# A chain of two transformer blocks on one core: halved first loads and identity products in the opening, another way of normalizing at the end

## The chip, the core and the metric

One core of one Trainium2 chip. The metric is the device time of one execution in microseconds (us). The kernel before takes 1332.92 us, the median of three runs from 1332.46 to 1334.28.

## The reference, cut to what matters

The input x is 256 rows (tokens) of 1024 float32 values. Two blocks follow each other; all matrices are float32 and each is used once:

```python
x = first_block(x, ...)      # z = rms_norm(x, norm_g) @ w_in, retention, differential attention, w_out
h = x                        # second block, two layers
for layer in range(2):
    h = h + 0.5 * swiglu_ffn(rms_norm_2(h, ffn1_norm[layer]), ...)
    h = h + (conformer_conv(...) if layer < 1 else stick_breaking_attention(...) @ attn_w_o)
    h = h + 0.5 * swiglu_ffn(rms_norm_2(h, ffn2_norm[layer]), gate, up, down)
return rms_norm_2(h, final_norm)   # h * rsqrt(mean(h * h) + 1e-6) * g
```

The change touches the two ends: the road from x to the first products with w_in, and the road from the last products (the down matrix of the last ffn) through the last residual and the last rms norm to the output.

## The kernel before, in words

Products are made from pairs of float32r parts: a value is split into a rounded part (hi) and the remainder (lo), and three products hi·hi, lo·hi, hi·lo are summed in PSUM. The weights come as a stream of 208 slabs, each four 128-row tiles of 512 columns (1 MB, two DMAs of 512 KB on SP's queue, `load`), in a ring of four slots (`raw`, `whi`, `wlo`). For every slab ACT makes the rounded part (`cast`, line 1092, signal `hi_ready`), DVE the remainder (`low`, line 1384, signal `lo_ready`), each two slabs ahead of TensorE, and TensorE runs 24 products of 512 columns: four tiles, two token tiles t of 128, three parts (`slab`, `part`, lines 595 to 597). A slot is loaded again when its remainder is made and rounded again when TensorE has used it (`half_done`).

Opening. SP loads x in two DMAs of 512 KB (one for each token tile), then the slabs. ACT loads the gain of the first norm, TensorE transposes it (line 736). TensorE then waits for x and transposes it in four fills (`fill`, line 673), each four 128x128 transposes into one of the two banks `tp`; a fill gives two of the eight k tiles. ACT scales each by the gain and rounds it (`fill_hi`, line 1105), DVE makes the remainder (`fill_lo`, line 1399). A third fill needs the first one's remainder. Both engines do two fills, then slab 0, then two fills, then slab 1. The norm's root factor is applied to results later: DVE collects statistics of x after slab 1 (`stats_half`, `stats_close`) and POOL makes the root (`residual_rs`), after which POOL issues its small loads. The order of the first slabs is (chunk 0, lower k), (chunk 1, lower k), (chunk 0, upper k), (chunk 1, upper k), so slabs 0 and 1 need k tiles 0 to 3 alone, which are the left half of x. `GAIN_STEP`, `LAM_STEP` say at which slab the other gains and small vectors are used.

End. The last ffn (`ffn2b`) has 11 down slabs. The left 512 output columns are complete in the middle of slab 5; DVE adds them to h (`residual`, line 1433) and takes their statistics. The last slab holds four k tiles for the right 512 columns: 12 products for t = 0, then 12 for t = 1. For each t DVE adds the right half to h (line 1962), takes statistics of it and joins them (lines 1415 to 1971), POOL makes the root in two steps (lines 429 and 433), DVE multiplies both halves by root and gain (line 1978), and SP stores each half of a tile, four stores of 256 KB (line 404). SP ends when all have landed.

`KEEP_WARM` (line 955, in the middle of the kernel) is a block of 22 products of 128x128 float32 whose results nobody reads. At line 1281 ACT loads the table set of the square root, and lines 1292 and 1301 use Square and Sqrt.

## Time and profile before

| | us |
|---|---|
| median of three timed runs | 1332.92 |
| span of the profiled execution | 1330.2 |
| TensorE busy in it | 1306.7 (98%) |
| DVE busy | 873.8 (66%) |
| ACT busy | 625.0 (47%) |
| POOL busy | 100.3 (8%) |

The profiled execution's own time runs from its first to its last instruction, 1330.2 us, and is 2.7 us under the median of the timed runs; the rest lies around the span. A busy time adds up the instructions of an engine; TensorE's are pipelined, so their starts lie nearer together than they are long, and the distance of starts is what a product costs in a stream. The timeline gives start, duration, engine, line and operands, and in brackets how long the engine had been idle and what released it. The chain of waits goes back from the last instruction, each piece to what released it.

### The profile page before, as it was taken

What the parts mean: (1) busy time and instruction counts of PE and PEld (TensorE: products, weight loads), DVE (VectorE), ACT (ScalarE), POOL (GpSimd) and SP (SyncE); (2) the same over time, 40 slices, a digit from 0 to 9 for tenths busy, and PEclk for the clock granted to TensorE, in tenths of its full rate; (3) what the DMA queues carried; (4) which work ended last, traced back from release to release, by engine and by line L of the source; (5) the groups of instructions that cost most, each with busy time, mean ns of one, the idle gap of its engine ahead of it and who ended that gap; (6) DMA issues with size and microseconds to landing.
All of it is one profiled execution on the core that took longest, in us unless ns stands there. A gap on an engine that the chain in (4) does not pass through costs nothing.

```text
span 1330.2 us, 17856 instructions
## 1 busy us (share of the span) xinstructions
PE 1306.7 (98%) x7374; PEld 1130.3 (85%) x7374; DVE 873.8 (66%) x988; ACT 625.0 (47%) x760; POOL 100.3 (8%) x141
## 2 busy tenths in 40 slices
PE   7999999999999999999999999999999999999997
PEld 5888877888888888899888888998888887988886
DVE  5565676767677655886777755557775566777753
ACT  5255576524455533325455543345554355455540
POOL 4123011001000002110000000000000010100000
PEclk9999999999999999999999999999999999999999
DMA  9544535456656655310455574545556422565540
GB/s 317 164 165 162 178 127 154 163 191 198 211 181 194 209 192 195 127 64 1 159 172 190 188 235 165 190 159 186 190 188 228 159 96 83 186 218 190 186 166 32
DMA packets 164911, 224.82 MB, mean 169 GB/s; under 512 B 7473, under 2 KB 105857, under 8 KB 164832
## 3 DMA queue, kind: packets, MB, share of 16 engines
q1 hardware_dynamic: 163168, 220.23, 50.3%
q0 software_dynamic: 1648, 3.47, 1.0%
q8 instruction: 58, 0.95, 0.3%
q14 instruction: 21, 0.17, 0.0%
q10 hardware_dynamic: 16, 0.00, 0.0%
HBM read 222.62 MB, written 1.05 MB: 168 GB/s over the span
## 4 chain that ended last, share of the span: by engine, by line
PE 94%; DVE 3%; ACT 2%; DMA 0%; issue 0%; POOLq 0%; DVEq 0%; POOL 0%; SPq 0%; ACTq 0%
PE acc L652 14%; PE acc L595 14%; PE acc L597 14%; PE acc L596 14%; PE att L652 8%; PE acc L650 7%; PE att L650 4%; PE att L891 4%; PE acc L626 2%; PE acc L630 2%; PE acc L628 2%; PE tp L673 1%; ACT pre L1310 1%; DVE wlo L1384 1%; ACT whi L1092 0%; DVE wexp L1938 0%
## 5 line engine op out<-in xcount | busy, mean ns | idle before, releaser
L1384 DVE TENSOR_TENSOR wlo<-raw,whi 128x2048 fp32r<-128x2048 f32 x208 | 474.6, 2290 | 167.9 <-ACT whi L1092 167.8
L1092 ACT ACTIVATE whi<-raw 128x2048 fp32r<-128x2048 f32 x208 | 395.0, 1913 | 102.4 <-PE acc L597 92.2
L652 PE MATMUL acc<-aT,whi 128*128 128x512 f32 x832 | 290.9, 391 | 0.0
L650 PE MATMUL acc<-aT,wlo 128*128 128x256 f32 x832 | 233.6, 281 | 0.0
L652 PEld LDWEIGHTS acc<-aT,whi 128*128 128x128 f32 x832 | 155.6, 187 | 33.8
L595 PE MATMUL acc<-whi,aT 128*128 128x512 f32 x448 | 179.6, 401 | 3.7 <-DVE wlo L1384 2.0
L597 PE MATMUL acc<-wlo,aT 128*128 128x512 f32 x448 | 175.8, 392 | 0.0
L596 PE MATMUL acc<-whi,aT 128*128 128x512 f32 x448 | 175.7, 392 | 0.0
L652 PE MATMUL att<-aT,whi 128*128 128x512 f32 x448 | 157.8, 391 | 0.0
L650 PEld LDWEIGHTS acc<-aT,wlo 128*128 128x128 f32 x832 | 157.3, 189 | 0.0
L595 PE MATMUL acc<-whi,hT_hi 128*128 128x512 f32 x352 | 137.3, 390 | 0.0
L596 PE MATMUL acc<-whi,hT_lo 128*128 128x512 f32 x352 | 137.0, 389 | 0.0
L597 PE MATMUL acc<-wlo,hT_hi 128*128 128x512 f32 x352 | 136.9, 389 | 0.0
L650 PE MATMUL att<-aT,wlo 128*128 128x256 f32 x448 | 125.4, 280 | 0.0
L595 PEld LDWEIGHTS acc<-whi,aT 128*128 128x128 f32 x448 | 85.1, 190 | 22.2 <-issue 3.5
L597 PEld LDWEIGHTS acc<-wlo,aT 128*128 128x128 f32 x448 | 85.1, 190 | 18.1
L652 PEld LDWEIGHTS att<-aT,whi 128*128 128x128 f32 x448 | 83.8, 187 | 18.4
L596 PEld LDWEIGHTS acc<-whi,aT 128*128 128x128 f32 x448 | 85.2, 190 | 16.5
L1227 ACT ACTIVATE low_part<-acc 128x512 f32<-128x512 f32 x52 | 31.0, 596 | 124.4 <-PE acc L652 124.4
L1105 ACT ACTIVATE aT<-tp,gain 128x256 fp32r<-128x256 f32 x72 | 28.3, 475 | 123.4 <-PE tp L673 123.4
L650 PEld LDWEIGHTS att<-aT,wlo 128*128 128x128 f32 x448 | 84.7, 189 | 0.0
L597 PEld LDWEIGHTS acc<-wlo,hT_hi 128*128 128x128 f32 x352 | 66.1, 188 | 13.8
(306 smaller groups left out, 1737.7 us busy)
## 6 DMA issues: line engine op xcount, KB each, us to landing
raw<-in_ffn_w_gate_dram SPq DMA_DIRECT2D x88, 512.0 KB, 3.8
raw<-in_ffn_w_up_dram SPq DMA_DIRECT2D x88, 512.0 KB, 4.9
raw<-in_ffn_w_down_dram SPq DMA_DIRECT2D x88, 512.0 KB, 4.7
raw<-in_w_in_dram SPq DMA_DIRECT2D x72, 512.0 KB, 4.6
raw<-in_conv_w_pw_dram SPq DMA_DIRECT2D x24, 512.0 KB, 4.7
raw<-in_w_kv_dram SPq DMA_DIRECT2D x16, 512.0 KB, 5.0
raw<-in_ret_w_o_dram SPq DMA_DIRECT2D x8, 512.0 KB, 4.8
raw<-in_diff_w_o_dram SPq DMA_DIRECT2D x8, 512.0 KB, 4.4
```

What stands on the lines that cost most here:

```text
L595: mm_(banks[t][:, :], tokens(Th, kt, t), hi_, start=first_ and j == 0, stop=False)
L596: mm_(banks[t][:, :], tokens(Tl, kt, t), hi_, start=False, stop=False)
L597: last = mm_(banks[t][:, :], tokens(Th, kt, t), lo_, start=False, stop=last_ and j == len(kts) - 1)
L626: mm_(dst, whi[:, slot, cols], aT_hi[:, kt, :], start=half == 0 and j == 0 and n == 0, stop=False, skip_group_check=True)
L628: mm_(dst, whi[:, slot, cols], aT_lo[:, kt, :], start=False, stop=False, skip_group_check=True)
L650: mm_(bank[:, 0:T], wlo[:, slot, cols], aT_hi[:, kt, :], start=half == 0 and j == 0, stop=False, skip_group_check=True)
L652: last = mm_(bank[:, :], whi[:, slot, cols], aT[:, kt, :, :].rearrange("p a n -> p (a n)"), start=False, stop=half == 1 and j == SLAB_K - ...
L891: last = mm_(att[i % 2][:, 0:P], wm[:, i % WM_BUFS, d_ * P:(d_ + 1) * P], uT[:, i, PADN - d_:PADN - d_ + P], start=d_ == 0, stop=d_ == SHI ...
L1092: A_(whi[:, slot, :], raw[:, slot, :], ACT.Copy).then_inc(hi_ready, 1)
L1105: last = A_(dst[:, kt, :], tp[b % 2][:, q * T:(q + 1) * T], ACT.Copy, scale=gain[:, GROW[g] + kt:GROW[g] + kt + 1])
L1227: A_(low_part[:, up, :, :], ffn_pair(name, c, up)[:, :, T:CW], ACT.Copy)\
L1384: V.tensor_tensor(wlo[:, slot, :], raw[:, slot, :], whi[:, slot, :].bitcast(F32), ALU.subtract)\
```

## The change

Opening. x is loaded in halves of its columns: the left halves of both token tiles (2 x 256 KB), then slab 0, then the right halves, then slab 1. TensorE does ten 128x128 float32 products of the identity with itself (`stay_busy`) between the gain's transpose and the wait for x, and ten more behind the first two fills. Slab 0 is rounded and its remainder made in two halves (two k tiles each), and TensorE begins its first 12 products when the top half and the first fill are there. The fills of the right half of x stand behind slab 0 on TensorE, and behind the work for slab 2 on ACT and DVE; statistics of the left half stand ahead of slab 1's remainder, those of the right half behind the fills.

End. DVE takes no statistics in the last ffn. ACT loads the table set with Sqrt ahead of the down slabs of `ffn2b`, squares the left half of h with a running sum as soon as it is there, then DVE multiplies the left half by the gain. The last 12 products of 512 columns become 24 of 256: columns 512 to 767 first, then 768 to 1023 in another bank (`last_columns`). DVE adds the right half of t = 0, that of t = 1 as far as it is there, and the last 256 columns when they are done; ACT sums squares and makes the square root (scale 1/sqrt(1024) in the squares, the left sum and 1e-6 as bias), DVE the reciprocal. ACT scales and stores the left halves from its own queue, DVE weights the right halves and SP stores them. POOL's root for the output is gone. The padding `align` shrinks by what the new small tiles take.

```diff
+            def x_half(n, landed_):
+                cols = slice(n * CW, (n + 1) * CW)
+                for t in range(TT):
+                    sp_.dma_start(h[:, t, cols], A["x"][0, t * P:(t + 1) * P, cols]).then_inc(landed_, 16)
+
+            x_half(0, x_left)
...
-                    sp_.dma_start(dst, src).then_inc(landed[k % SLOTS], 16)
+                    sp_.dma_start(dst, src).then_inc(top_landed if (k, q) == (0, 0) else landed[k % SLOTS], 16)
...
-            square(0, w_in, [(W_IN_COLS[c], half) for c, half in start[:4]])
-
-            square(4, w_in, [(W_IN_COLS[c], half) for c, half in start[4:]])
+            square(0, w_in, [(W_IN_COLS[c], half) for c, half in start[:1]])
+            x_half(1, x_right)
+            square(1, w_in, [(W_IN_COLS[c], half) for c, half in start[1:]])
...
-                    sp_.wait_ge(out_ready, 2 * t + n + 1)
-                    sp_.dma_start(out[0, t * P:(t + 1) * P, cols], h[:, t, cols]).then_inc(out_landed, 16)
+                sp_.wait_ge(out_ready, t + 1)
+                sp_.dma_start(out[0, t * P:(t + 1) * P, CW:D], h[:, t, CW:D]).then_inc(out_landed, 16)
...
-                pool.wait_ge(stat_ready, RS_OUT + t + 1)
-                tile = rs_tmp[:, RS_OUT, t:t + 1]
-                rsqrt(rs[:, RS_OUT, t:t + 1], tile, tile, 1.0, EPS, rs_ready)
...
+            def last_columns(slot, banks, kt0):
+
+                for n in range(2):
+                    to = slice(n * FW, (n + 1) * FW)
+                    for j in range(SLAB_K):
+                        cols = slice(j * CW + n * FW, j * CW + (n + 1) * FW)
+                        hi_, lo_ = natural(hT_hi, kt0 + j, 1), natural(hT_lo, kt0 + j, 1)
+                        mm_(banks[n][:, to], hi_, whi[:, slot, cols], start=n == 1 and j == 0, stop=False)
+                        mm_(banks[n][:, to], lo_, whi[:, slot, cols], start=False, stop=False)
+                        last = mm_(banks[n][:, to], hi_, wlo[:, slot, cols], start=False, stop=j == SLAB_K - 1)
+                    last.then_inc(last_done, 1)
...
+                            if name == "ffn2b" and s == DOWN_SLABS - 1 and t == 1:
+                                last_columns(k % SLOTS, (acc[g % 2][t], att[0]), 2 * q0)
+                                break
...
-            pe.wait_ge(x_landed, 32)
-            for b in range(4):
+
+            def stay_busy(n):
+                for _ in range(n):
+                    mm_(att[1][:, 0:P], ident[:, :], ident[:, :], start=True, stop=True)
+
+            stay_busy(10)
+            pe.wait_ge(x_left, 32)
+            for b in range(2):
                 fill(b, of(h), (2 * b, 2 * b + 1))
-
+            stay_busy(10)
...
-                if s in (0, 1):
-                    pe.wait_ge(tp_lo, 2)
-                elif s == 2:
+                if s == 0:
+                    for q, (made, needed) in enumerate(((top_lo, 1), (lo_ready, 1))):
+                        pe.wait_ge(tp_lo, q + 1)
+                        pe.wait_ge(made, needed)
+                        for t in range(TT):
+                            last = part(acc[0], aT_hi, aT_lo, 0, 2 * q, (2 * q, 2 * q + 1), t, q == 0, False)
+                            if q == 1:
+                                last.then_inc(half_done, 1)
+                    pe.wait_ge(x_right, 32)
+                    for b in range(2, 4):
+                        fill(b, of(h), (2 * b, 2 * b + 1))
+                    continue
+                if s == 2:
...
-                act.wait_ge(landed[slot], 32 * (k // SLOTS + 1))
+                act.wait_ge(landed[slot], 32 * (k // SLOTS + 1) - (16 if slot == 0 else 0))
...
-                for b in (2 * k, 2 * k + 1):
-                    fill_hi(b, aT_hi, (2 * b, 2 * b + 1), "norm_g")
-                cast(k)
+            for b in range(2):
+                fill_hi(b, aT_hi, (2 * b, 2 * b + 1), "norm_g")
+            top, bottom = slice(0, SLAB_K * CW // 2), slice(SLAB_K * CW // 2, SLAB_K * CW)
+            act.wait_ge(top_landed, 16)
+            A_(whi[:, 0, top], raw[:, 0, top], ACT.Copy).then_inc(top_hi, 1)
+            act.wait_ge(landed[0], 16)
+            A_(whi[:, 0, bottom], raw[:, 0, bottom], ACT.Copy).then_inc(hi_ready, 1)
+            cast(1)
...
+                if s == 0:
+                    for b in range(2, 4):
+                        fill_hi(b, aT_hi, (2 * b, 2 * b + 1), "norm_g")
...
+                if not gain_out:
+                    nc.scalar.preload_act_table_set("sqrt_and_others")
...
+            squared = [act_out[:, t, :, :].rearrange("p f n -> p (f n)") for t in range(TT)]
+
+            def sum_squares(t, i, cols):
+
+                to = slice(cols.start % CW, cols.start % CW + cols.stop - cols.start)
+                A_(squared[t][:, to], h[:, t, cols], ACT.Square, scale=D ** -0.5,
+                   accum_out=last_ss[:, t, i:i + 1]).then_inc(last_sq, 1)
+
+            def deviation(t, i, n):
+
+                act.wait_ge(sum_ready, t + 1)
+                act.wait_ge(last_sq, n)
+                A_(last_std[:, t:t + 1], last_ss[:, t, i:i + 1], ACT.Sqrt, bias=last_sum[:, t:t + 1]).then_inc(last_dev, 1)
+
+            def left_out(t):
+
+                act.wait_ge(last_rs, t + 1)
+                A_(h[:, t, 0:CW], h[:, t, 0:CW], ACT.Copy, scale=last_scale[:, t:t + 1]).then_inc(out_left, 1)
+                act.wait_ge(out_left, t + 1)
+                act.dma_start(out[0, t * P:(t + 1) * P, 0:CW], h[:, t, 0:CW]).then_inc(out_landed, 16)
+
+            left = PLACE["ffn2b"].g + FC
+            for t in range(TT):
+                act.wait_ge(acc_free, 2 * left + t + 1)
+                sum_squares(t, 0, slice(0, CW))
+            act.wait_ge(last_res, 1)
+            sum_squares(0, 1, slice(CW, D))
+            deviation(0, 1, 3)
+            act.wait_ge(last_res, 2)
+            sum_squares(1, 1, slice(CW, CW + FW))
+            left_out(0)
+            act.wait_ge(last_res, 3)
+            sum_squares(1, 2, slice(CW + FW, D))
+            deviation(1, 2, 5)
+            left_out(1)
...
+            for part_, made, sig in ((slice(0, SLAB_K * CW // 2), top_hi, top_lo),
+                                     (slice(SLAB_K * CW // 2, SLAB_K * CW), hi_ready, lo_ready)):
+                dve.wait_ge(made, 1)
+                V.tensor_tensor(wlo[:, 0, part_], raw[:, 0, part_], whi[:, 0, part_].bitcast(F32), ALU.subtract)\
+                    .then_inc(sig, 1)
             for t in range(TT):
-                for n in range(2):
-                    stats_half(t, n)
-            stats_close(RS_X)
+                stats_half(t, 0)
+            low(1)
...
+                if s == 0:
+                    for b in range(2, 4):
+                        fill_lo(b, aT_hi, aT_lo, (2 * b, 2 * b + 1), "norm_g")
+                    for t in range(TT):
+                        stats_half(t, 1)
+                    stats_close(RS_X)
...
-            for t in range(TT):
-                done(w.k + FFN_SLABS - 1, t)
-                cols = h[:, t, CW:D]
-                step(V.scalar_tensor_tensor(cols, acc[(w.g + FC + 1) % 2][t][:, :],
-                                            rs_down[:, RS_F2B, t:t + 1], cols, ALU.mult, ALU.add))
-                sync()
-                stats_half(t, 1)
-                sync()
-                step(V.bn_aggr(mv[:, t, :], stats[:, t, :, :]))
-                sync()
-                step(V.tensor_tensor(msq[:, t:t + 1], mv[:, t, 0:1], mv[:, t, 0:1], ALU.mult))
-                sync()
-                V.tensor_tensor(rs_tmp[:, RS_OUT, t:t + 1], msq[:, t:t + 1], mv[:, t, 1:2], ALU.add)\
-                    .then_inc(stat_ready, 1)
+            bank = acc[(w.g + FC + 1) % 2]
+
+            def last_residual(t, cols, from_):
+
+                to = h[:, t, cols]
+                V.scalar_tensor_tensor(to, from_[:, cols.start - CW:cols.stop - CW], rs_down[:, RS_F2B, t:t + 1], to,
+                                       ALU.mult, ALU.add).then_inc(last_res, 1)
+
+            def inverse(t):
+
+                dve.wait_ge(last_dev, t + 1)
+                V.reciprocal(last_scale[:, t:t + 1], last_std[:, t:t + 1]).then_inc(last_rs, 1)
+                dve.wait_ge(last_rs, t + 1)
+
             dve.wait_ge(gout_landed, 16)
             for t in range(TT):
-                dve.wait_ge(rs_ready, RS_OUT + t + 1)
-                for n in range(2):
-                    cols = slice(n * CW, (n + 1) * CW)
-                    V.scalar_tensor_tensor(h[:, t, cols], h[:, t, cols], rs[:, RS_OUT, t:t + 1], g_out[:, cols],
-                                           ALU.mult, ALU.mult).then_inc(out_ready, 1)
+                dve.wait_ge(last_sq, t + 1)
+                V.tensor_tensor(h[:, t, 0:CW], h[:, t, 0:CW], g_out[:, 0:CW], ALU.mult).then_inc(left_by_g, 1)
+            V.tensor_scalar(last_sum[:, 0:1], last_ss[:, 0, 0:1], EPS, None, ALU.add).then_inc(sum_ready, 1)
+
+            done(w.k + FFN_SLABS - 1, 0)
+            last_residual(0, slice(CW, D), bank[0])
+            dve.wait_ge(last_done, 1)
+            last_residual(1, slice(CW, D), bank[1])
+            inverse(0)
+            right = h[:, 0, CW:D]
+            V.scalar_tensor_tensor(right, right, last_scale[:, 0:1], g_out[:, CW:D], ALU.mult, ALU.mult)\
+                .then_inc(out_ready, 1)
+            dve.wait_ge(last_sq, 4)
+            V.scalar_tensor_tensor(last_sum[:, 1:2], last_ss[:, 1, 0:1], EPS, last_ss[:, 1, 1:2], ALU.add, ALU.add)\
+                .then_inc(sum_ready, 1)
+            dve.wait_ge(last_done, 2)
+            last_residual(1, slice(CW + FW, D), att[0])
+            inverse(1)
+            right = h[:, 1, CW:D]
+            V.scalar_tensor_tensor(right, right, last_scale[:, 1:2], g_out[:, CW:D], ALU.mult, ALU.mult)\
+                .then_inc(out_ready, 1)
```


## Rows read from the trace of the kernel before

**Rows 1.** The page, busy time, share of the span and instructions of TensorE.

```profile
PE 1306.7 (98%) x7374; PEld 1130.3 (85%) x7374; DVE 873.8 (66%) x988; ACT 625.0 (47%) x760; POOL 100.3 (8%) x141
```

**Rows 2.** Chain of waits at the start: start us, us, what.

```profile
1.24 4.52 DMA h<-in_x_dram
...
7.02 1.63 ACT aT L1105 x4
8.64 1.81 ACT whi L1092
10.48 2.30 DVE wlo L1384
```

**Rows 3.** Timeline 0:21 (start us, us, engine, line, what) and x's DMA to landing.

```profile
0.79 0.59 ACTq L1124 DMA_DIRECT2D attw<-in_norm_g_dram  x1
...
3.34 0.24 PE L736 MATMUL att<-ident,attw 8*128 8x8 f32 x1 [3.34 <-DMA attw<-in_norm_g_dram]
...
5.80 1.97 PE L673 MATMUL tp<-ident,h 128*128 128x128 f32 x8 [2.22 <-DMA h<-in_x_dram]
...
7.98 1.66 DVE L1399 SCALAR_TENSOR_TENSOR aT<-tp,gain,aT 128x256 fp32r<-128x256 f32 x4 [4.20 <-ACT aT L1105]
...
12.91 0.77 PE L595 MATMUL acc<-whi,aT 128*128 128x512 f32 x1 [2.04 <-DVE wlo L1384]
...
13.89 1.91 ACT L1092 ACTIVATE whi<-raw 128x2048 fp32r<-128x2048 f32 x1 [0.19 <-DMA raw<-in_w_in_dram]
...
17.32 0.51 PE L596 MATMUL acc<-whi,aT 128*128 128x512 f32 x1
...
17.67 0.39 PE L597 MATMUL acc<-wlo,aT 128*128 128x512 f32 x1
...
20.64 0.39 PE L595 MATMUL acc<-whi,aT 128*128 128x512 f32 x1
...
DMA to landing us min/median/max: 3.7/4.1/4.5
```

**Rows 4.** Windows: busy us of each engine, then granted clock, DMA share, GB/s.

```profile
12.00:14.00 2.00, 1.08 (x3) 0.92 (x4) 2.00 (x5) 1.81 (x2) 0.00 (x0) 1.00 1.05 386
```

**Rows 5.** Line 955, identity-like products: duration ns min/median/max, first and last start.

```profile
L955 PE MATMUL att<-meanw x44: 275/275/275, 614.1 to 618.9; 128*128 128x128 f32 x44
```

**Rows 6.** Timeline of the end, DVE and SP, and the stores' landing.

```profile
1271.43 6.70 DVE L1384 TENSOR_TENSOR wlo<-raw,whi 128x2048 fp32r<-128x2048 f32 x3 [1.11 <-ACT whi L1092]
...
1319.73 0.75 DVE L1962 SCALAR_TENSOR_TENSOR h<-acc,rs_down,h 128x512 f32<-128x512 f32 x1 [14.74 <-PE acc L597]
...
1322.45 0.75 DVE L1962 SCALAR_TENSOR_TENSOR h<-acc,rs_down,h 128x512 f32<-128x512 f32 x1 [0.61 <-PE acc L597]
...
1324.40 0.16 DVE L1971 TENSOR_TENSOR rs_tmp<-msq,mv 128x1 f32<-128x1 f32 x1
...
1326.34 1.42 DVE L1978 SCALAR_TENSOR_TENSOR h<-h,rs,g_out 128x512 f32<-128x512 f32 x2 [0.45 <-POOL rs L433]
...
1325.26 2.86 SPq L404 DMA_DIRECT2D out_dram<-h  x4
...
DMA to landing us min/median/max: 2.0/2.1/2.1
```

**Rows 7.** 256-column products in the timeline; groups of ACT (mean ns).

```profile
332.75 0.28 PE L626 MATMUL acc<-aT,whi 128*128 128x256 f32 x1
...
334.91 0.28 PE L626 MATMUL acc<-aT,whi 128*128 128x256 f32 x1
...
L1236 ACT ACTIVATE hT_hi<-hid 128x512 fp32r<-128x512 f32 x44 | 27.6, 627 | 13.1 <-DVE hid L1666 13.1
...
L1207 ACT ACTIVATION_READ_ACCUMULATOR prob<-prob,nmx 128x1 f32 x32 | 6.0, 189 | 0.0
```

**Rows 8.** Timeline of ACT in the convolution: root behind squares (line 1292), table load.

```profile
614.92 0.31 ACT L1301 ACTIVATE rdev<-sdev 128x128 f32<-128x128 f32 x1 [1.22 <-DVE sdev L1848]
615.25 1.28 ACT L1302 ACT_TABLE_LOAD   x1
```

More of the change, by code:

```diff
@@ L259, in build @@
         small_landed = sem("small_vectors_landed")
-        x_landed = sem("x_landed")
+        x_left = sem("x_left_landed"); x_right = sem("x_right_landed")
+        top_landed = sem("first_top_landed"); top_hi = sem("first_top_high"); top_lo = sem("first_top_low")
         x_again = sem("x_again")
@@ L568, in _ @@
                            .to_broadcast([P, D])).then_inc(gout_landed, 16)
-            for t in range(TT):
-                pool.wait_ge(stat_ready, RS_OUT + t + 1)
-                tile = rs_tmp[:, RS_OUT, t:t + 1]
-                rsqrt(rs[:, RS_OUT, t:t + 1], tile, tile, 1.0, EPS, rs_ready)
         @block.tensor
@@ L1425, in stats_close, with residual @@
                 V.tensor_tensor(rs_tmp[:, use, :], msq[:, :], mv[:, :, 1], ALU.add).then_inc(stat_ready, 1)
-            def residual(g, n, scale, ready, banks=None):
+            def residual(g, n, scale, ready, banks=None, summed_here=True):
                 for t in range(TT):
```

30 lines of the change are left out of this document (16 added, 14 removed).

## The prediction

> **What bounds the kernel now.** I read the page first: TensorE is busy 98% of the span [rows 1], so the middle of the program is a stream of products and only what delays its first one, slows it, or lies behind its last one can be won. So I read the chain of waits at the start [rows 2], the timeline of the opening [rows 3], and the timeline of the end [rows 6]. The change leaves everything else as it is.
>
> At the start the reader should follow one chain: x landed 5.76 (1.24 + 4.52), transposes from 5.80, four scalings on ACT 7.02 to 8.65, rounding of slab 0 to 10.44, its remainder on DVE 10.48 to 12.78, first slab product 12.91 [rows 2, 3]. Then the products: ten starts from 12.91 to 17.32 are 0.44 apart, the thirteen from 17.67 to 20.64 are 0.228 apart [rows 3]. The granted-clock column reads 1.00 in the slow stretch too [rows 4], so it doesn't show this; by the spacing the first ten ran at the lower of TensorE's levels (1.2 GHz) and the rest at the upper (2.4 GHz). The level rose at about 17.6, that is 4.7 after the first product of an unbroken stream; the two bursts of eight transposes before it ended without a rise. Cost of the low level before: 4.7 less half of it, 2.3. Slab 1 began at 20.64; that is the figure for the opening that I carry.
>
> At the end, products for tokens 0 to 127 were done at 1319.70 and all at 1322.42 (the releases of the two DVE residuals), DVE's last product with the gain ended at 1327.76, the last store was issued about 1327.8 and landed 2.1 later, and the span closed at 1330.2 [rows 6]. So the tail behind TensorE is 7.8.
>
> **Opening, part by part.** *Halved x and slab.* 512 KB of x landed 3.7 after its issue [rows 3], so x_left should be there at about 4.5, 1.3 earlier than all of x; by the rate of the later slabs (1 MB in 2.7: slab 2 at 13.85 [rows 3], three MB behind x at 5.76) the top half of slab 0 is there by 6, the bottom by 7.3. Nothing below waits for either.
>
> *First identity block.* It stands between the gain's transpose (start 3.34) and the transposes of x, in TensorE's order, so x's transposes queue behind it. 22 such products are recorded as 44 of which the first and last starts lie 4.8 apart, 0.112 each at the upper level [rows 5]; a transpose is one record, and eight of them took 1.97 with the last one 0.42 long, 0.221 each at the lower level [rows 3]. So ten products are 20 records: 20 x 0.221 = 4.4 at the lower level, from 3.6 to 8.0. This is later than x_left's 4.5 and than the old start 5.80: what halving x wins is lost again, and 2.2 more. The unbroken stream now starts at 3.6; with the same 4.7 the level rises at 8.3, within the transposes. I bound the rise by 7.0 (some earlier phase of whatever decides it) and 10.5 (2.2 later). First four transposes done: 8.8 at 8.3 (0.22 + 3 x 0.11 + 0.27 for the last one's end, rounded up), 8.05 at 7.0, 9.1 if it stays low.
>
> *From the transposes to the first product.* Four scalings 1.63 on ACT, then half a slab: 1.81 for 2048 columns becomes about 0.95; DVE's own four scalings end 2.67 after the transposes (9.64 against 6.97 [rows 2, 3]), which is level with ACT's half, then half of 2.30, 1.2, and 0.14 to TensorE: 4.05 where it was 5.94. So 8.8 + 4.05 = 12.85 for the first product, nearly the 12.91 of before (12.1 to 13.15). The bottom half is ready 1.2 later, when TensorE is still in its 12 x 0.227 = 2.7 of products for the top. The second identity block (20 records, 2.2 at the upper level) runs from about 9.5 to 11.7, in TensorE's idle time.
>
> *Slab 0 and the right half.* 24 products x 0.227 = 5.45, then eight transposes of x_right, formerly ahead of the start and now inside the stream: 8 x 0.112 = 0.9. Slab 1 starts at 12.85 + 5.45 + 0.9 = 19.2 against 20.64: gain 1.4 (2.2 with the early rise, 1.1 with the rise at 10.5). Its data is in time: DVE makes slab 1's remainder after the bottom half and two statistics (5.05 + 1.3 + 2.3 = 8.65 after the transposes), TensorE wants it 10.4 after. The fills of x_right on ACT and DVE and the rest of the statistics come before slab 3's remainder; it is made by about 25.5 and wanted at 30. The statistics close about 3 later, so POOL's root and its small loads do; TensorE first meets them through accumulators that have a slab of slack. I cost all that at nothing; without that slack it would be up to 1.
>
> **End, part by part.** *Left half ahead, squares, root.* ACT has been idle since its last cast, so squares of the left half and DVE's weighting of it are hidden. The table load ahead of the down slabs costs ACT 1.28 [rows 8]; the three remainders from 1271.43 [rows 6] are for slabs that TensorE begins at 1278.9, 1284.3 and 1289.8 (1322.42 less 5.44 a slab), so 1.28 is hidden with over 2 to spare. Square and Sqrt run on one table: in the convolution the root (614.92) follows line 1292's squares with no load between, the load comes behind it [rows 8].
>
> *Split columns.* 24 products of 256 columns instead of 12 of 512: eighteen such starts lie 2.16 apart, 0.120 each [rows 7], so 2.88 for 2.72. In the clock of before: first half 1321.14, all 1322.58.
>
> *The chain.* DVE residual of tile 0 to 1320.5; ACT squares 512 (0.63 plus 0.1 and a 0.19 read of the sum [rows 7]) to 1321.4, root (0.2 to 0.31) to 1321.65; DVE residual of tile 1 to 1321.92, reciprocal (0.16 to 0.21, as one-column steps [rows 6]) to 1322.1, weighting right 0 to 1322.86, a sum of one column to 1323.06; residual of the last 256 columns (0.42 to 0.48, a quarter of 1.66 [rows 3]) to 1323.55. ACT meanwhile: squares of 256 to 1322.6, left 0 scaled to 1323.2, its store issued until 1323.85 (0.59 was ACT's issue of the gain [rows 3]), only then the last squares (0.69, to 1324.55) and root (1324.8); DVE reciprocal 1325.0, right 1 weighted 1325.77. SP issues at 1325.8; ACT issues the last left store at 1325.7. Were ACT held by a store of its own until that lands (2.1 instead of 0.59), the end would gain 0.5. Before, the last issue was at 1327.8 with the same landing behind it: gain 2.0. With ACT free of its store's 0.3 (hand-over and issue overlapped), 2.4; with 0.1 more on each of eight hand-overs, 1.2.
>
> **Sum.** Opening 1.4 (1.1 to 2.2), end 2.0 (1.2 to 2.4): 3.4 off a span of 1330.2, which stands 2.7 below the median 1332.92 of the timed runs, so 1329.5 (1328.3 to 1330.6). Of this kernel a difference of about 0.2% (2.7 us) can be told from none: faster means below 1330.25.
>
> A rule that speaks against the opening: the Trainium skill, "TensorE: Matmul & The Clock Gate", Part 4 (PE-mode transpose), says that transposes don't count as busy for the clock gate in the way products do. The two bursts of transposes that ended at the lower level agree, though they are short and broken. By that rule the transposes of x cut the stream of identity products in two, and rival A's time, 1332.5 to 1333.2, takes the place of 1329.5.
>
> **Rivals.** *A, the level doesn't rise ahead of slab 0.* Block one to 8.0, transposes at the lower level to 9.8, block two 4.4 more to 14.2, and that holds up the first product (its data is ready at 13.1). If the rise comes with the products at about 17.6 to 18.9, slab 0 costs 5.45 + 1.7 to 2.35 and slab 1 starts at 14.2 + 7.15 + 0.9 = 22.3 to 22.9: opening loses 1.6 to 2.3. For it: the bursts of transposes without a rise. Against: block one alone is 4.4 of unbroken products. With the end's 2.0: 1332.5 to 1333.2, no measurable change.
>
> *B, slower: the level stays low for all of slab 0.* The queue of A starts slab 0 at 14.2; if the rise then takes longer than the 4.7 of before, because the waits for the half slabs cut the stream, 24 products at 0.427 end at 24.4, the eight transposes take 1.8 and slab 1 starts at 26.2, 5.6 late: 1332.9 + 5.6 - 2.0 = 1336.5. From a rise at 18.3 on, the opening loses the 2.0 of the end and the kernel is slower; a measurable 2.7 needs 23.7, twice the old 4.7 after its first product. Against it: the bottom half is ready before TensorE has done the top, so nothing cuts that stream.
>
> *C, identity products cost half.* If ten are ten records, block one ends at 5.8, the first product comes at 11.1 and slab 1 at 17.5: opening 3.1, time 1327.8. The 44 records for 22 speak against.
>
> **How the numbers follow.** Forecast 0.6, A 0.27, B 0.06, C 0.07. Below 1330.25 falls nearly all of the forecast (0.85 of it) and C: 0.58. Slower by over 0.2%: most of B, 0.04. The rest, 0.38, within. The range takes the forecast, C and A: 1327.5 to 1333.2.
>
> **What would show it.** Right: 20 identity records from 3.6 to 8.0 and transposes behind them; first slab product near 12.9 with starts 0.227 apart at once; slab 1 near 19.2; last store issued about 3.3 after TensorE's last product. Wrong: starts 0.43 apart from 14 to 18 (A) or to 24 (B), ACT's store over 0.6 (the end), transposes at 5.8 (C). If a rise comes inside block one, the opening gives up to 2.2; if TensorE waits anywhere between slab 1 and the last, a cover that I named is gone.

## The result, and the profile after

The changed kernel takes 1337.15 us (1336.3 to 1337.38, five runs) against 1332.92: ratio 1.0032, 95% interval 1.0019 to 1.0044. It is slower by 4.2 us where I forecast 3.4 less. The span of its profiled execution is 1335.4; that same execution took 1337.15, so 1.75 lie around the span.

The page, in the line that answers to [rows 1]: the granted clock is nearly the same (mean 0.998 before, 0.999 after), TensorE has 52 instructions more, and its busy time rose by 11.6 us.

```profile
PE 1318.3 (99%) x7426; PEld 1135.5 (85%) x7426; DVE 871.1 (65%) x984; ACT 631.4 (47%) x776; POOL 96.8 (7%) x137
```

The opening, which answers to [rows 2, 3] (timeline: start us, us, engine, line, what):

```profile
2.68 0.24 PE L756 MATMUL att<-ident,attw 8*128 8x8 f32 x1 [2.68 <-POOL rel L435]
2.85 4.64 PE L760 MATMUL att<-ident 128*128 128x128 f32 x20
...
7.28 1.34 PE L678 MATMUL tp<-ident,h 128*128 128x128 f32 x8
8.28 1.57 ACT L1141 ACTIVATE aT<-tp,gain 128x256 fp32r<-128x256 f32 x4 [5.58 <-PE tp L678]
...
12.20 0.47 PE L600 MATMUL acc<-whi,aT 128*128 128x512 f32 x1 [1.35 <-DVE wlo L1536]
...
13.41 1.92 ACT L1128 ACTIVATE whi<-raw 128x2048 fp32r<-128x2048 f32 x1 [1.67 <-DMA raw<-in_w_in_dram]
...
18.54 0.47 PE L600 MATMUL acc<-whi,aT 128*128 128x512 f32 x1
```

The identity block works: the first slab product comes at 12.20 with the next ones 0.23 apart at once, and slab 1 begins at 18.54 where it was 20.64. The opening gained 2.1. The end (answers to [rows 6]) has TensorE's last product, DVE's last weighting and ACT's last store:

```profile
1329.09 0.28 PE L700 MATMUL att<-wlo,hT_hi 128*128 128x256 f32 x1
...
1330.96 0.29 ACT L1420 ACTIVATE last_std<-last_ss,last_sum 128x1 f32<-128x1 f32 x1
1331.29 0.16 DVE L2061 RECIPROCAL last_scale<-last_std 128x1 f32<-128x1 f32 x1 [1.22 <-ACT last_std L1420]
...
1331.49 0.75 DVE L2085 SCALAR_TENSOR_TENSOR h<-h,last_scale,g_out 128x512 f32<-128x512 f32 x1
1332.24 0.35 ACTq L1427 DMA_DIRECT2D out_dram<-h  x1
```

The view of the output's tile says when the four stores landed:

```profile
DMA to landing us min/median/max: 2.1/2.5/2.7
```

From 1329.37 to 1335.4 the tail behind TensorE is 6.0, where it was 7.8. So both ends gained, and yet TensorE's last product ended 7.0 later. The loss lies in between, where the prediction had looked at nothing. I laid the starts of the down stages of the four ffns (the first product that reads `hT_hi`) side by side:

| start of, us | before | after | difference |
|---|---|---|---|
| slab 1 | 20.64 | 18.54 | -2.1 |
| down stage 1 | 441.83 | 441.00 | -0.8 |
| down stage 2 | 767.76 | 768.83 | +1.1 |
| down stage 3 | 999.31 | 1002.33 | +3.0 |
| down stage 4 | 1262.37 | 1267.35 | +5.0 |
| TensorE's last product | 1322.02 | 1329.09 | +7.1 |

Each down stage costs 1.9 to 2.1 more (the last with the split columns), and 1.3 more go before the first one. The windows view of the first down stage, before and then after (window, its length, busy us and count of TensorE, its weight loads, DVE, ACT, POOL; granted clock, DMA share, GB/s):

```profile
441.83:502.61 60.78, 60.78 (x273) 50.38 (x272) 33.32 (x25) 26.28 (x20) 0.00 (x0) 1.00 0.60 202
```

```profile
441.00:503.71 62.71, 62.71 (x273) 50.56 (x272) 33.33 (x25) 26.29 (x20) 0.00 (x0) 1.00 0.59 196
```

The same 273 instructions, TensorE busy without a gap in both, full clock in both, the same work on DVE and ACT, and 1.93 us more. So TensorE waited for nobody; its products themselves came slower. The groups of this stage (count | busy us, mean ns | idle) show it on the same products, before and then after:

```profile
L595 PE MATMUL acc<-whi,hT_hi 128*128 128x512 f32 x88 | 34.3, 390 | 0.0
```

```profile
L600 PE MATMUL acc<-whi,hT_hi 128*128 128x512 f32 x88 | 35.0, 397 | 0.0
```

The timeline of four products in a row, again before and then after, shows by how much:

```profile
1290.29 0.39 PE L595 MATMUL acc<-whi,hT_hi 128*128 128x512 f32 x1
1290.51 0.39 PE L596 MATMUL acc<-whi,hT_lo 128*128 128x512 f32 x1
1290.74 0.39 PE L597 MATMUL acc<-wlo,hT_hi 128*128 128x512 f32 x1
1290.96 0.39 PE L595 MATMUL acc<-whi,hT_hi 128*128 128x512 f32 x1
```

```profile
1289.84 0.40 PE L600 MATMUL acc<-whi,hT_hi 128*128 128x512 f32 x1
1290.08 0.39 PE L601 MATMUL acc<-whi,hT_lo 128*128 128x512 f32 x1
1290.31 0.40 PE L602 MATMUL acc<-wlo,hT_hi 128*128 128x512 f32 x1
1290.55 0.40 PE L600 MATMUL acc<-whi,hT_hi 128*128 128x512 f32 x1
```

Three products take 0.67 before and 0.71 after. Over all down products (some 350 starts of each kind) the mean distance is 0.226 to 0.228 before and 0.234 to 0.235 after; the 192 products that read `bT_hi` and `bT_lo` in the first block went from 0.2295 to 0.2363 in the mean. Products on `aT` kept their 0.228. The sum, an estimate, is 1056 x 0.0073 + 192 x 0.0068 = 9.0.

Is it other traffic to SBUF? Ahead of the last products there is a stretch in which no other engine works and DMAs move 1 GB/s at most. The windows view of 12 us of it, before and then after:

```profile
1307.00:1319.00 12.00, 12.00 (x54) 9.93 (x54) 0.00 (x0) 0.00 (x0) 0.00 (x0) 1.00 0.00 0
```

```profile
1313.00:1325.00 12.00, 12.00 (x53) 9.62 (x52) 0.00 (x0) 0.00 (x0) 0.00 (x0) 1.00 0.01 1
```

The starts in these two stretches are still 0.227 and 0.234 apart. So neither DMAs nor the other engines slow the products; only what TensorE itself reads and writes is left.

What do `hT` and `bT` have that `aT` has not? They lie in SBUF, the core's on-chip memory, behind the tile `align`. The addresses of the allocation (bytes in a partition):

```
                     before    after
whi                   49280    49280
wlo                   82048    82048
aT                   123008   123008
end of dqk_s         140968   141096
hT_hi                152192   152288
hT_lo                174720   174816
```

The allocation starts each tile at a multiple of 32 bytes. The four new small tiles (24, 8, 8 and 8 bytes) take 4 x 32 = 128 bytes, while `align` from 112 to 100 columns gives back 448 - 416 = 32 (400 bytes, rounded up). So all that lies behind `align` moved by 96 bytes. That `align` "shrinks by what the new small tiles take", as I wrote ahead of the prediction, was false.

### The profile page after: what moved, and what is told of

Its sections match the earlier page's. It is cut to its first block, busy times and chain, and to the rows that moved or that the text cites. A ratio compares the mean times of both kernels' runs of the same rounds, so it can differ in the third digit from the quotient of the medians.

```text
span 1335.4 us, 17973 instructions
## 1 busy us (share of the span) xinstructions
PE 1318.3 (99%) x7426; PEld 1135.5 (85%) x7426; DVE 871.1 (65%) x984; ACT 631.4 (47%) x776; POOL 96.8 (7%) x137
## 4 chain that ended last, share of the span: by engine, by line
PE 94%; DVE 3%; ACT 2%; issue 0%; POOL 0%; ACTq 0%; DVEq 0%; POOLq 0%
PE acc L657 14%; PE acc L600 14%; PE acc L602 14%; PE acc L601 14%; PE att L657 8%; PE acc L655 7%; PE att L655 4%; PE att L927 4%; PE acc L631 2%; PE acc L635 2%; PE acc L633 2%; PE tp L678 1%; ACT pre L1355 1%; DVE wlo L1465 1%; DVE wexp L2029 0%
## 5 line engine op out<-in xcount | busy, mean ns | idle before, releaser
L602 PEld LDWEIGHTS acc<-wlo,aT 128*128 128x128 f32 x448 | 84.4, 188 | 17.8
```

The lines of the kernel that those rows point to most:

```text
L602: last = mm_(banks[t][:, :], tokens(Th, kt, t), lo_, start=False, stop=last_ and j == len(kts) - 1)
```

## The experiments

The theory in the expectations is P, placement: where `hT` and `bT` lie sets how far apart their products start. The rival is that the products are slower for another reason of the changed program. In the diffs `align` is the only edit unless more is shown. Times in us; "shift" is that of `hT` and `bT` against before.

| run | edit | median (range, runs) | ratio to before [95%] | first down stage, first to last start |
|---|---|---|---|---|
| before | | 1332.92 | | 60.55 |
| after | shift 96 | 1337.15 (1336.3-1337.38, 5) | 1.0032 [1.0019, 1.0044] | 62.48 |
| e1_aligned | after, shift 0 | 1328.0 (1327.55-1328.6, 5) | 0.9963 [0.995, 0.9975] | 60.55 |
| e2_before_shifted | before, shift 96 | 1342.2 (1341.27-1343.41, 4) | 1.007 [1.0056, 1.0083] | 62.48 |
| e3_shift_64 | after, shift 64 | 1335.92 (1335.41-1336.48, 10) | 1.0022 [1.0013, 1.0031] | 62.24 |
| e5_minus_128 | after, shift -128 | 1336.0 (1334.94-1336.19, 10) | 1.0023 [1.0013, 1.0032] | 62.23 |
| e9_minus_256 | after, shift -256 | 1328.2 (1327.94-1328.79, 5) | 0.9966 [0.9953, 0.9979] | 60.55 |
| e10_weights_moved | `hT` as before, weights +128 | 1335.47 (1334.96-1335.87, 10) | 1.0021 [1.0011, 1.0031] | 62.23 |
| e11_all_moved | `hT` -128, weights +128 | 1327.61 (1327.31-1328.44, 4) | 0.9962 [0.9947, 0.9976] | 60.54 |
| e4_no_identity | e1 without both blocks | 1328.83 (1328.33-1329.69, 6) | 0.9969 [0.9957, 0.9981] | |
| e6_opening_alone | e1 with the old end | 1330.13 (1329.67-1330.56, 11) | 0.9978 [0.9969, 0.9987] | |
| e7_whole_x | e1, x in whole rows | 1327.86 (1327.35-1328.46, 5) | 0.9962 [0.995, 0.9975] | |
| e8_better | e7 and three edits | 1326.29 (1326.23-1326.64, 5) | 0.9952 [0.9939, 0.9964] | |
| e12_one_block | e8 without its second block | 1327.52 (1327.0-1328.35, 4) | 0.996 [0.9946, 0.9975] | |

**Is it the placement?** One edit in the changed kernel, and the opposite one in the kernel before:

```diff
-        sb("align", [P, 100])
+        sb("align", [P, 80])
```

> The whole change, with the padding align at 80 columns instead of 100, so that every tile behind it lies at the address that it had in the kernel before (a multiple of 64 bytes in each partition; in the changed kernel 32 behind one). Theory P (placement): the products whose stationary operand is hT_hi or hT_lo start 0.234 apart in the changed kernel and 0.227 before; there are 11 x 24 x 4 = 1056 of them, 8.0 us, and 192 with bT about 1.4. Then this run has 0.227 again and takes 1337.15 - 9.4 = 1327.8. Rival N (the new code itself slows TensorE, by its DMAs, its clock or another order): starts stay 0.234 apart and the time stays 1337.

```diff
-        sb("align", [P, 112])
+        sb("align", [P, 132])
```

> The kernel before with align at 132 columns instead of 112, nothing else: the tiles behind it lie 96 bytes further, as in the changed kernel. Theory P: the down slabs' products start 0.234 apart, time 1332.9 + 9.4 = 1342.3. Rival N: 0.227 and 1332.9.

Both came as placement says: 1328.0 and 1342.2. Twenty columns of a tile that nobody reads or writes take 9.2 from the changed kernel, and as many more put 9.3 on the old one. The timeline of e1_aligned has the old distance back, three products in 0.67:

```profile
1290.02 0.39 PE L600 MATMUL acc<-whi,hT_hi 128*128 128x512 f32 x1
1290.24 0.39 PE L601 MATMUL acc<-whi,hT_lo 128*128 128x512 f32 x1
1290.47 0.39 PE L602 MATMUL acc<-wlo,hT_hi 128*128 128x512 f32 x1
1290.69 0.39 PE L600 MATMUL acc<-whi,hT_hi 128*128 128x512 f32 x1
```

**Which addresses are good?** Columns of `align` 96, 48 and 16:

> The whole change with align at 96 columns: the tiles behind it lie 64 bytes further than in the kernel before, again a multiple of 64. If the distance from a multiple of 64 bytes counts: 0.227 apart and the time of the aligned kernel, 1327.8. If it is the very address, or what else shares a region with it: 0.234 and 1337.

> The whole change with align at 48 columns: the tiles behind it lie 128 bytes below their addresses in the kernel before, where hT_hi begins at a multiple of 128 bytes (152192). A shift by 96 gave starts 0.234 apart, one by 64 gave 0.233. If the position within 128 bytes is what counts: 0.227 apart and the aligned kernel's 1328.0. If only the very addresses of before are good (256 bytes, or what lies beside them): 0.233 and about 1336.

> The whole change with align at 16 columns: tiles behind it 256 bytes below their addresses in the kernel before. Shifts by 96, 64 and -128 were all slow (starts 0.232 to 0.235 apart). Every fast stage so far has the stationary tile (hT_hi, hT_lo, aT) and the weights (whi, wlo) at 128 behind a multiple of 256. Theory P256: position within 256 bytes decides, so this is fast: 0.227 and 1328.0. If only the old addresses themselves are good: 0.233 and 1336.

That a multiple of 64 is enough fell (1335.9, not 1327.8), and so did a multiple of 128 (1336.0, not 1328). A shift of 256 is as good as none, 1328.2. All bad shifts cost nearly the same: 60.55 in the down stage becomes 62.24 for 64 bytes, 62.23 for 128 and 62.48 for 96. In e5_minus_128 `hT_hi` begins at 152064, itself a multiple of 256, and is slow; so if an address counts by itself, it isn't "be a multiple of 256".

**Own address or distance?** Before, the distance between `hT_hi` and `whi` is 102912 = 402 x 256, that of `hT_lo` 125440 = 490 x 256, of `wlo` to `whi` 32768, of `aT` 73728 = 288 x 256. To part the two, a tile of 128 bytes stands ahead of the weights, and `align` is cut so that `hT` is back at its old address, or moves along:

```diff
+        sb("lead", [P, 32])
         raw = sb("raw", [P, SLOTS, SLAB_K * CW])
...
-        sb("align", [P, 100])
+        sb("align", [P, 48])
```

> The whole change with an unused tile of 128 bytes ahead of raw and align at 48 columns: raw, whi, wlo, h and aT lie 128 bytes further (multiples of 256), hT and all behind align at the old addresses (128 behind a multiple). If the stationary tile's own address counts: products on hT stay at 0.227, those on aT slow down to 0.233 (some 890 recorded ones of that form, 5 to 6 us): 1333 to 1334. If the distance between stationary and moving tile counts (modulo 256): aT stays at 0.227, hT goes to 0.233 to 0.234, and the time is about 1336.

The second has `align` at 16 columns:

> As the one with the weights moved, but align at 16 columns, so hT and the tiles behind it are moved too, to multiples of 256: all by 128 bytes against each other as in the kernel before. If the distance counts: all at 0.227 and 1328.0. If the own address counts: hT at 0.233 and aT too, about 1341.

In both runs the weights, `aT` and all else ahead of `align` lie 128 bytes further than before. In e10_weights_moved `hT` is at its old address; in e11_all_moved it is 128 bytes below it. So the two tiles did not move by the same amount there, whatever its name says: they moved in opposite directions, and their distance changed by 256. The addresses of the seven placements:

```
                     whi    hT_hi  distance  over a multiple of 256  down stage
before, e1         49280   152192    102912                       0       60.55
after, e2          49280   152288    103008                      96       62.48
e3_shift_64        49280   152256    102976                      64       62.24
e5_minus_128       49280   152064    102784                     128       62.23
e10_weights_moved  49408   152192    102784                     128       62.23
e9_minus_256       49280   151936    102656                       0       60.55
e11_all_moved      49408   152064    102656                       0       60.54
```

The same address of `hT_hi` is fast and slow: 152192 in e1_aligned (1328.0) and e10_weights_moved (1335.5), 152064 in e11_all_moved (1327.6) and e5_minus_128 (1336.0). The same distance gives the same stage wherever the tiles lie. And the products on `aT`, which moved along with the weights in e10_weights_moved, kept their 0.228 there. Four products of each at the same place, e10_weights_moved and then e11_all_moved:

```profile
1290.12 0.40 PE L601 MATMUL acc<-whi,hT_hi 128*128 128x512 f32 x1
1290.35 0.39 PE L602 MATMUL acc<-whi,hT_lo 128*128 128x512 f32 x1
1290.58 0.40 PE L603 MATMUL acc<-wlo,hT_hi 128*128 128x512 f32 x1
1290.82 0.39 PE L601 MATMUL acc<-whi,hT_hi 128*128 128x512 f32 x1
```

```profile
1289.81 0.39 PE L601 MATMUL acc<-whi,hT_hi 128*128 128x512 f32 x1
1290.04 0.39 PE L602 MATMUL acc<-whi,hT_lo 128*128 128x512 f32 x1
1290.26 0.39 PE L603 MATMUL acc<-wlo,hT_hi 128*128 128x512 f32 x1
1290.49 0.39 PE L601 MATMUL acc<-whi,hT_hi 128*128 128x512 f32 x1
```

0.70 against 0.68 for three. What counts is the distance between the tile loaded into TensorE (`hT`, the stationary side) and the one streamed through it (the weights), and among the seven placements, which have five distances, it is good where it is a multiple of 256 bytes. `raw`, `h` and `aT` moved with the weights too, but nothing reads or writes them in the quiet stretch above, where the slow starts remain.

**What are the parts worth, once placed well?** These runs start from e1_aligned.

```diff
-            stay_busy(10)
             pe.wait_ge(x_left, 32)
             for b in range(2):
                 fill(b, of(h), (2 * b, 2 * b + 1))
-            stay_busy(10)
```

> The aligned change without the two blocks of identity products. If the blocks raise TensorE's level early (they end before the first slab product, whose starts were 0.23 apart at once): without them x's transposes start about 4.5 instead of 7.3, the first slab product about 9.6, at the lower level for some 4.6; slab 0 ends about 17, slab 1 starts at 17.9 or so, bounded by its remainder (slab 1 was rounded only from 13.4, when it landed). Then the time is 0.5 below the aligned kernel's, the blocks cost as much as they bring. If the level only rises later, or slab 1 is later: up to 2 above it.

Missed: I expected it half a microsecond below e1_aligned and it is 0.8 above (the two ranges overlap only from 1328.3 to 1328.6). The transposes start at 4.89, the first product comes at 10.66, 1.1 earlier than with the blocks, but the first eight products are slow, and slab 1 begins at 18.70 against 18.17. Timeline of e4_no_identity:

```profile
4.89 1.97 PE L678 MATMUL tp<-ident,h 128*128 128x128 f32 x8 [1.97 <-DMA h<-in_x_dram]
...
8.20 1.06 ACT L1165 ACTIVATE whi<-raw 128x1024 fp32r<-128x1024 f32 x1 [0.47 <-DMA raw<-in_w_in_dram]
...
10.66 0.77 PE L600 MATMUL acc<-whi,aT 128*128 128x512 f32 x1 [3.80 <-DVE wlo L1534]
11.22 0.63 PE L601 MATMUL acc<-whi,aT 128*128 128x512 f32 x1
...
13.78 0.61 PE L601 MATMUL acc<-whi,aT 128*128 128x512 f32 x1
14.21 0.42 PE L602 MATMUL acc<-wlo,aT 128*128 128x512 f32 x1
```

I had expected the first product at 9.6 and it came 1.1 later: x_left landed at 4.89 instead of 4.5, and ACT waited 0.47 for the top half of slab 0 (second row), which landed at 8.2, not at 6 as I had worked out. The rest of the difference to e1_aligned is the eight slow products: 8.04 from the first product to slab 1, against 6.43.

e6_opening_alone is e1_aligned with the end of the kernel before (statistics, POOL's root, four stores on SP).

> The new opening with the end of the kernel before, all tiles at their old addresses. In the aligned kernel slab 1 began at 18.17, against 20.64 before; its level rose within the first identity block. Theory: the opening gives 2.4 of the aligned kernel's 4.9, so 1330.5 here, and the new end the other 2.5 in this comparison (1.8 by the spans behind TensorE's last product, from 7.8 to 6.0). If the end gives its 1.8 only: 1329.8. If the opening gives less in time than slab 1's start says: above 1331.

Measured 1330.13, between the two values: by the medians the opening gives 2.8 (2.7 against the 1332.84 that the kernel before took beside this run) and the end the other 2.1. The spans say a little less for the end: 1327.6 against 1326.4, with slab 1 at 17.83 in the first and 18.17 in the second, so 1.2 + 0.3 = 1.5; about half of the rest lies outside the span (see "Around the span"). Both lie in the range I had for it, 1.2 to 2.4.

```diff
-            x_half(0, x_left)
+            for t in range(TT):
+                sp_.dma_start(h[:, t, :], A["x"][0, t * P:(t + 1) * P, :]).then_inc(x_left, 16)
...
-            x_half(1, x_right)
...
-                    pe.wait_ge(x_right, 32)
```

> The aligned change with x loaded whole again (two DMAs of 512 KB ahead of slab 0), all else as in the aligned kernel. Theory: halving x wins nothing, since x's transposes stand behind the first identity block (it ended at 7.1 in the aligned kernel; x whole lands at 5.8), and it costs order: slab 1 was rounded from 13.87 on, when it landed, where 3 MB should be there at about 11.2. Slab 1 then starts at 18.0 to 18.2 as before, bounded by TensorE, and the time is the aligned kernel's 1328.0 within 0.3. Rival: the smaller first load is needed, and the time rises by 1 or more.

Measured 1327.86 against 1328.0: halving x is worth nothing while TensorE runs the first block until 7.3, after all of x has landed. It also brings slab 1 later, though nothing waited for that here: in the changed kernel ACT waits for slab 1 until 13.41 (13.87 in e1_aligned), in e7_whole_x it casts it at 11.61 without a wait.

e8_better puts the findings together: x whole, a first block of six that ends when x lands, the fills of the right half behind the second block, and tile 0's left store taken off ACT's queue.

```diff
-            stay_busy(10)
+            stay_busy(6)
             pe.wait_ge(x_left, 32)
...
             stay_busy(10)
+            for b in range(2, 4):
+                fill(b, of(h), (2 * b, 2 * b + 1))
...
                 sp_.dma_start(out[0, t * P:(t + 1) * P, CW:D], h[:, t, CW:D]).then_inc(out_landed, 16)
+                if t == 0:
+                    sp_.wait_ge(out_left, 1)
+                    sp_.dma_start(out[0, 0:P, 0:CW], h[:, 0, 0:CW]).then_inc(out_landed, 16)
```

> A version meant to beat both: x whole; first identity block of 6 products instead of 10 (2.8 to about 5.5), so that x's transposes start when x lands (5.8); the transposes of the right half behind the second block, in TensorE's idle time, instead of behind slab 0; at the end the store of tile 0's left half is issued by SP instead of ACT. First slab product at 10.75 (11.74 in the aligned kernel), slab 1 at 16.3 to 16.5 (18.17), the last squares on ACT 0.3 earlier: 2.0 below the aligned kernel, 1326.0. If six products and four transposes don't keep the stream that raises the level: starts 0.43 apart behind 10.7, slab 1 near 18.2 and 1327.8.

Measured 1326.29, 6.6 below the kernel before and 10.9 below the changed one. Slab 1 begins at 16.59, 1.6 earlier than in e1_aligned, and the tail behind TensorE is 5.9 instead of 6.15; together they are the 1.8 between the two spans. What the smaller block and the moved fills give one by one was not run. The last question was whether its second block is needed:

> The better version (1326.3) without its second block of ten identity products. The level had risen at about 8.3 there, inside the second block. If the second block is needed to raise it: slab 0's first products 0.43 apart from about 10.9 on, for up to 4.5, 10 of them 0.2 longer: 2.0 above, 1328.3. If the transposes count too and the level rises by 9: 1326.3.

It is, though for less than the 2.0 that I had written: 1327.52, 1.2 above e8_better. The first product comes at 10.77, a little earlier than the 11.04 of e8_better, but five products are slow and slab 1 begins at 17.45. Timeline of e12_one_block, products before and behind the rise:

```profile
12.61 0.63 PE L599 MATMUL acc<-whi,aT 128*128 128x512 f32 x1
13.04 0.45 PE L600 MATMUL acc<-wlo,aT 128*128 128x512 f32 x1
13.33 0.40 PE L598 MATMUL acc<-whi,aT 128*128 128x512 f32 x1
13.56 0.40 PE L599 MATMUL acc<-whi,aT 128*128 128x512 f32 x1
```

## Why the prediction was wrong, point by point

**The step that failed** is the last sentence of its first paragraph, "The change leaves everything else as it is". I had the four new tiles and the smaller `align` in the diff and took their cost as nothing, without working out one address. The term measured is +9.2 (1337.15 - 1328.0). The parts are -2.8 for the opening, -2.1 for the end and +9.2 for the placement. They add up to the measured 4.2 but for rounding, as they must, since they are differences of the same medians; what supports the 9.2 independently is the 9.3 of e2_before_shifted and the 9.0 from the starts. Without the placement the forecast would have been right in direction and small in size: 4.9 less instead of 3.4, just under its 1328.3. None of the rivals had it: A, B and C all turn on TensorE's level in the opening, and B, the slower one, asked for starts 0.43 apart to 24, which didn't come. My last condition, "if TensorE waits anywhere between slab 1 and the last, a cover that I named is gone", looked in the right stretch for the wrong sign: TensorE never waited, its products came further apart. The chance of 0.04 for slower was far too low for a sum whose 1290 us in the middle were assumed and not worked out.

**First block.** Predicted 20 records from 3.6 to 8.0, found 2.85 to 7.28. The length is right; it started earlier since the gain's transpose came at 2.68, not 3.34. I had the rise at 8.3, "within the transposes", and so it was: by the records one by one, twenty identity records and the first three transposes start 0.213 apart (but for the very first), and from 7.9 on they start 0.110 apart. By the group it is 1.34 for eight transposes where [rows 3] had 1.97 at the lower level and 1.04 is the time at the upper one (the rows of 17.75 after and of e1_aligned). Earlier start and earlier rise make the gain 2.1 in this profile where I had 1.4, with 2.2 as the end of the range; the 2.7 to 2.8 of the medians is beyond it, and the opening is the second term that was mis-sized. Rivals A and B fell with that, and C with the 20 records.

What I had not foreseen is that the moment of the rise differs between profiles of programs that do the same up to there. Counted from the block's first record it came after 5.1 in the changed kernel, 4.2 in e1_aligned, 5.5 in e7_whole_x and 3.2 in e6_opening_alone. Over all nine profiles with these two blocks it came 3.1 (e3_shift_64, e9_minus_256) to 6.2 (e5_minus_128) after. That the rise at 7.9 came so near the 8.3 that I forecast from one profile's 4.7 was therefore in part luck. It alone moves slab 1 (18.54, 18.17, 18.47 and 17.83; 17.8 to 18.8 over the nine), so where such runs differ by less than a microsecond in the opening of one profile, the median decides, not the profile. The same holds for the kernel before: its 20.64 is one draw, and e2_before_shifted, with the same opening, has slab 1 at 22.62, with the first product 1.4 later and thirteen slow products instead of ten. That can be why the profile says 2.1 for the opening and the medians 2.8; it isn't shown. Timeline of e1_aligned and then of e7_whole_x, transposes behind the block:

```profile
7.12 1.04 PE L678 MATMUL tp<-ident,h 128*128 128x128 f32 x8
```

```profile
7.07 1.56 PE L673 MATMUL tp<-ident,h 128*128 128x128 f32 x8
```

**The rule on transposes.** First the rows: in the changed kernel and in e7_whole_x the level rose between one transpose and the next, 5.1 and 5.5 after the block began, with no product in between. In e12_one_block a block of six ended 0.2 before the transposes, and the level rose at the second of them: 1.26 for eight. Then TensorE had 1.55 without work, and the level fell again inside the next eight, which took 1.74; that, and not a rise that never came, is why its first slab products were slow.

```profile
5.92 1.26 PE L676 MATMUL tp<-ident,h 128*128 128x128 f32 x8 [0.23 <-DMA h<-in_x_dram]
...
8.74 1.74 PE L676 MATMUL tp<-ident,h 128*128 128x128 f32 x8 [1.55 <-DVE aT L1478]
```

The Trainium skill, "TensorE: Matmul & The Clock Gate", Part 4, says that the full clock doesn't engage for transposes, since they don't count as busy in the way products do. These traces disagree with the first half: a rise arrives in the middle of transposes, and they then run at the upper level, 0.110 apart. On the second half they are open. In e5_minus_128 all eight transposes stayed at the lower level and the rise came with the second block's first record, 6.2 after the first block began, and the slab's products were fast all the same, because that block is then over by 11.4, before they start at 12.43. Rival A had it run at the lower level, to 14.2. Whether transposes alone can bring a rise about isn't shown: the bursts before the first slab in the kernel before and in e4_no_identity ended without one.

**Transposes to the first product.** Predicted 4.05 from the fourth transpose; from ACT's start at 8.28 it was 3.92, to 12.20. The second block, in TensorE's idle time, took 2.4 (8.45 to 10.85) and held up nobody.

**Halved x.** Predicted x_left at 4.5 and the halves of slab 0 at 6 and 7.3. In e4_no_identity, where nothing hides it, they landed at 4.89, 8.2 and 9.5. I had taken the rate of whole slabs ([rows 3]); the halved loads moved less. The window 4 to 6 us has 285 GB/s after (first row) against 399 before (second row); e1_aligned and e4_no_identity, halved too, have 254 and 323, and e7_whole_x, with x in whole rows again, 342:

```profile
4.00:6.00 2.00, 2.00 (x12) 2.00 (x10) 0.00 (x0) 0.00 (x0) 0.00 (x0) 1.00 0.91 285
```

```profile
4.00:6.00 2.00, 0.20 (x1) 0.20 (x2) 0.00 (x0) 0.00 (x0) 0.00 (x0) 1.00 1.01 399
```

It cost nothing in the changed kernel, since the first block and the fills end later still.

**End.** The chain came as predicted, step by step, and two sizes were off. ACT's issue of its store took 0.38, not 0.59, so the last squares began 0.99 after TensorE's end where I had 1.27, and the last issue came 2.9 after it where I had 3.2. Against that, the four stores, two from each of two queues, landed in 2.1 to 2.7 instead of 2.0 to 2.1. Split columns cost 0.26 (59.65 to 59.91 from first to last start of the stage, before and e1_aligned; 0.16 predicted). So the tail gains 1.8 less 0.26, and 2.1 by the times.

**Around the span.** I put 2.7 between span and median and took it to stay. The changed kernel's own times are 1.7 to 1.8 over their spans, and so are those of all runs with the new end (up to 1.85). The kernel before has 1.7 to 2.4, by the run, and e6_opening_alone, with the old end, 1.7 to 2.1. So about 0.3 of the end's gain lies outside the span (medians 1.98 in e6_opening_alone and 1.70 in e1_aligned), which I had at nothing; what it is isn't shown. The remaining 0.3 to 0.9 of the 2.7 is that the profiled execution of the kernel before was quicker than the median.

## What to carry to other kernels

A change that adds or resizes a tile moves every tile behind it: work out the addresses before and after, and keep the distance between what TensorE loads and what it streams as it was, here a multiple of 256 bytes. When a profile shows the same instructions, no waits, full clock and a longer stretch, compare the distance of starts by the pair of tiles that the products read, and test with a padding tile alone. Products that only raise TensorE's level pay where they fill time in which it would wait anyway: the kernel takes 1328.8 with none, 1328.0 with ten ahead of the transposes and ten behind, and 1326.3 with six that end when x lands and with the later fills moved out of slab 0 (0.2 of this is the store moved at the end).

## What the hardware showed that I had not expected

- Products of 512 columns in float32r start 0.227 apart when stationary and streamed tile lie a multiple of 256 bytes apart (distances 102912 and 102656, the second with the tiles at two pairs of addresses), and 0.232 to 0.235 when the distance is off by 64, 96 or 128. That is 2.8% to 3.2% of a stage in which TensorE never waits. What in the chip does it isn't shown by these runs: the granted clock is 1.00 in both, and the weight loads take as long (50.4 and 50.6 us for 272). Other distances weren't tried.
- The 24 products of 256 columns at the end, on the same tiles, don't follow: they start 0.120 apart at the good distances (e1_aligned, e9_minus_256, e11_all_moved) and a little nearer together at the others, 0.118 at 128, 0.117 at 96 and 0.114 at 64. So "a multiple of 256 is good" is shown for the 512-column products alone.
- The Trainium skill, "SBUF — State Buffer", Operand start alignment, asks of a tile's start only a multiple of its element size, as a rule of what is allowed and not of speed. All placements here keep it, and they are 9.2 us apart.
- TensorE's level rose 3.1 to 6.2 after the first record of an unbroken stream of identity products and transposes, at another moment in each of nine profiles. After the first slab product of an opening without identity products it was 4.7 in the kernel before, 5.8 in e2_before_shifted and 3.5 in e4_no_identity. It fell again in e12_one_block after a pause of 1.55 and a few transposes.
- Four loads of 256 KB and two of 512 KB, issued between each other, moved 254 to 323 GB/s from 4 to 6 us in three profiles, where loads of 512 KB alone moved 342 and 399 in two, and the top half of slab 0 landed 2.2 later than worked out from the latter. Whether the size, the shorter rows or the order does it was not tried.
